# RWKV loop: identity products with a result in partitions 0 to 63 as TensorE transposes

## The reference, cut to what matters

```
def step(S, inp):
    r_t, w_t, k_t, v_t, kk_t, a_t = inp
    S = (S * w_t[:, :, None, :]
         - einsum('bhvk,bhk->bhv', S, kk_t)[..., None] * (kk_t * a_t)[:, :, None, :]
         + v_t[..., None] * k_t[:, :, None, :])
    return S, einsum('bhvk,bhk->bhv', S, r_t)
```

## Time and profile before

| what | us |
|---|---|
| median of 3 runs | 2818.54 |
| the runs | 2812.94 to 2820.93 |
| the profiled execution, its own time | 2810.1 |
| its span, first to last instruction | 2808.3 |

### The profile page before, as it was taken

The page is one execution under the profiler, slowest core; times in us unless marked ns, Lnnn a source line. Parts: engine busy times, 40 slices in busy tenths (PEclk is TensorE's granted clock), DMA queues, the critical chain, the costliest instruction groups (busy, mean ns, idle before and its releaser), DMA issues.

```text
span 2808.3 us, 63914 instructions
## 1 busy us (share of the span) xinstructions
PE 2549.5 (91%) x28913; PEld 2055.1 (73%) x28913; DVE 1173.8 (42%) x2014; ACT 558.0 (20%) x966; POOL 264.9 (9%) x166
## 2 busy tenths in 40 slices
PE   5899888999999979978888888888699999999993
PEld 3566556677776757747777777776599999999992
DVE  4434577544463376636655555627100000000004
ACT  3100221200010010024544444431200111011001
POOL 0000240000000000003333322210100000000001
PEclk9999999999999989979999999989799999999996
DMA  8554111312122013310000000002356555555553
GB/s 325 227 226 199 46 46 68 138 72 75 62 91 83 36 63 114 125 42 4 23 23 23 23 23 23 6 19 90 143 206 219 189 209 209 202 189 207 198 202 124
DMA packets 52552, 322.00 MB, mean 115 GB/s; under 512 B 8160, under 2 KB 10336, under 8 KB 21600
## 3 DMA queue, kind: packets, MB, share of 16 engines
q1 hardware_dynamic: 41824, 281.23, 27.4%
q10 hardware_dynamic: 7040, 20.45, 2.0%
q0 software_dynamic: 3456, 16.78, 1.5%
HBM read 289.07 MB, written 29.36 MB: 113 GB/s over the span
## 4 chain that ended last, share of the span: by engine, by line
PE 84%; DVE 7%; ACT 3%; issue 3%; DMA 2%; POOL 0%; SPq 0%; ACTq 0%; POOLq 0%; DVEq 0%
PE PS L877 35%; PE PS L1524 17%; PE PS L1539 8%; PE PS L1132 3%; PE PS L1265 3%; PE PS L1257 2%; PE PS L855 1%; PE PS L1197 1%; PE PS L1247 1%; PE PS L1329 1%; DMA arena<-in_k 1%; PE PS L598 1%; PE PS L1190 1%; ACT arena L1791 1%; PE PS L1224 1%
## 5 line engine op out<-in xcount | busy, mean ns | idle before, releaser
L877 PE MATMUL PS<-arena,ring 128*128 128x320 f32 x2680 | 752.0, 439 | 33.4 <-DVE arena L2389 12.3
L877 PEld LDWEIGHTS PS<-arena,ring 128*128 128x128 f32 x2680 | 512.6, 193 | 260.2 <-issue 24.7
L1524 PE MATMUL PS<-arena,ring 128*128 128x192 f32 x2816 | 465.5, 329 | 3.2 <-ACT arena L1906 3.2
L1524 PEld LDWEIGHTS PS<-arena,ring 128*128 128x128 f32 x2816 | 463.1, 192 | 4.2 <-ACT arena L1906 4.0
L1539 PE MATMUL PS<-arena,ring 128*128 128x192 f32 x1408 | 230.1, 326 | 0.0
L1539 PEld LDWEIGHTS PS<-arena,ring 128*128 128x128 f32 x1408 | 229.0, 190 | 0.0
L2639 DVE TENSOR_TENSOR arena<-arena,PS 128x192 f32<-128x192 f32 x88 | 31.2, 354 | 438.6 <-ACT arena L1912 438.6
L877 PE MATMUL PS<-arena 128*128 128x320 f32 x536 | 151.1, 432 | 0.0
L877 PEld LDWEIGHTS PS<-arena 128*128 128x128 f32 x536 | 101.8, 190 | 42.4
L796 POOL TENSOR_TENSOR arena<-arena,const 128x512 f32<-128x512 f32 (+1 forms) x24 | 26.2, 1091 | 1097.6 <-DVE arena L2490 765.2
L1265 PE MATMUL PS<-arena 64*64 64x64 f32 x3200 | 119.1, 220 | 10.9 <-issue 10.6
(11 more groups left out here) (331 smaller groups left out, 3130.6 us busy)
## 6 DMA issues: line engine op xcount, KB each, us to landing
ring<-in_k SPq DMA_DIRECT2D x145, 1024.0 KB, 4.8
arena<-in_k SPq DMA_DIRECT2D x48, 1024.0 KB, 9.1
ring<-in_exd SPq DMA_DIRECT2D x32, 1408.0 KB, 5.8
ring<-in_ffd SPq DMA_DIRECT2D x8, 1408.0 KB, 6.3
rkv_s<-arena ACTq DMA_DIRECT2D x24, 320.0 KB, 4.1
expert_rows<-arena POOLq DMA_DIRECT2D x4, 1536.0 KB, 10.3
x<-in_x SPq DMA_DIRECT2D x2, 2560.0 KB, 9.1
arena<-expert_rows ACTq DMA_DIRECT2D x8, 512.0 KB, 4.2
```

Source lines behind the costliest of these rows:

```text
L877: m = pe.matmul(out, lhs[:, k], rhs[:, k], start=k == 0, stop=k == count - 1)
L1524: m = pe.matmul(PS[:, k % 4, t * CAP:(t + 1) * CAP], w[:, kt, t * P:(t + 1) * P], xe[:, kt], start=kt == 0, stop=kt == KT - 1)
```

## The change

A helper `turned` sends an identity product to `pe.transpose` when its result lies in partitions 0 to 63, and to the same `pe.matmul` as before otherwise. It is put in for all four steps above. No wait, no buffer and no other engine's instruction is changed.

```diff
             wide = lambda b: psf[:, b * 512:b * 512 + TOK]
             eye_of = lambda hs: cst("eye64", hs)
 
+            def turned(out, rows, a, at):
+
+                if rows == heads[0]:
+                    return pe.transpose(out, a, eye_of(at))
+                return pe.matmul(out, a, eye_of(at), start=True, stop=True)
+
...
-                                m = pe.matmul(PS[token(c, h), b + r, k * HD:(k + 1) * HD], rkv[j % 2][hs, 2, c * HD:(c + 1) * HD], eye_of(hs), start=True, stop=True)
+                                m = turned(PS[token(c, h), b + r, k * HD:(k + 1) * HD], token(c, h), rkv[j % 2][hs, 2, c * HD:(c + 1) * HD], hs)
...
-                                    m = pe.matmul(PS[token(u, h), b + r, (2 * k + w) * HD:(2 * k + w + 1) * HD], KBf[hs, u, w], eye_of(hs), start=True, stop=True)
+                                    m = turned(PS[token(u, h), b + r, (2 * k + w) * HD:(2 * k + w + 1) * HD], token(u, h), KBf[hs, u, w], hs)
...
-                                m = pe.matmul(PS[hs, b + r, k * HD:(k + 1) * HD], QR[hs, u, 0], eye_of(hs), start=True, stop=True)
+                                m = turned(PS[hs, b + r, k * HD:(k + 1) * HD], hs, QR[hs, u, 0], hs)
...
-                            m = pe.matmul(PS[ts, 2 * i + r, k * HD:(k + 1) * HD], LTm[ts, 0, u], eye_of(ts), start=True, stop=True)
+                            m = turned(PS[ts, 2 * i + r, k * HD:(k + 1) * HD], ts, LTm[ts, 0, u], ts)
```

## The result

The changed kernel takes **3063.0 us**, the median of four runs (3057.1 to 3076.4), against 2816.4 for the kernel before on the same chip: a ratio of 1.0876, 95% interval [1.0856, 1.0897]. It is slower by 247 us, where 134 were forecast, and it lies above the range. The profiled execution took 3057.1 us, its span 3055.3.

The account below looks back on a forecast made before the run. PE was taken as the bound, at some 59 ns per pass of one array quarter. Changes of shape add 18.1 us per `j`, 145 in eight, less 11.7 of waits: 2818.5 + 134 = 2952 us, range 2920 to 3012.

Parts of the forecast that it names:

- the range: Whole kernel: the forecast's bounds, 2920 to 3012 us.
- The passes removed are worth nothing: In the four steps: removing 720 passes gains nothing, since the array quarters that stay set the same end.
- a quarter is the bound: In the four steps: each pass of one array quarter takes some 59 ns, and quarters run side by side.
- A transpose doesn't share the array with a 64*64 matmul: In the four steps: a 64x64 transpose runs as 64*128, so each change to or from a matmul is paid.
- Steps of under 60 ns: Sign of a wrong forecast: such steps between transposes and matmuls would make the time that of a rival.
- The first three rivals: Four steps: no shape change paid (2818 us, 0.10); saved passes count (2803, 0.05); serial, no change paid (2847, 0.06).
- The prices: Per `Q` pair 430 ns for 118, `KB` and `V` four 444 for 120, `first_inverse` four 618 for 236.
- the sum: RWKV loop: changes of shape add 18.1 us per `j`, 145 in eight, less 11.7 of waits, net +134 us.
- The waits: PE's waits for ACT's copies, 11.7 us, are swallowed; `var`'s (0.82) and `first_inverse`'s (0.55) stay.
- the clock falls: Rival, RWKV loop: mixed work at half clock adds some 100 us, 3050 us; chance 0.04.

Follow-up runs that it names:

- e11: Kernel before, matmuls only, products of each piece and of each `first_inverse` group sorted by array quarter: 2883.7 us, ratio 1.0250 to the kernel before.
- e2: The changed kernel in its order, each transpose replaced by a 128*64 matmul with half of the identity: 3089.1 us, ratio 1.0980 to the kernel before.
- e3: Kernel before with the transposes put into `Q` only: 2890.1 us, ratio 1.0263 to the kernel before.
- e4: Kernel before with the transposes put into `first_inverse` only: 2891.5 us, ratio 1.0269 to the kernel before.
- e9: The changed kernel with transposes in the third group alone (4 of the 20 units, none in `V`): 2877.8 us, ratio 1.0228 to the kernel before.
- e1: The changed kernel with all transposes of each piece and each `first_inverse` group issued before the matmuls: 2861.9 us, ratio 1.0174 to the kernel before.
- e7: Kernel before with transposes in `Q` only, ordered transpose, matmul, matmul, transpose: 2845.9 us, ratio 1.0114 to the kernel before.
- e8: Kernel before, no transposes, with products of `change_sides` put between those of `first_inverse`, behind each pair of units: 2806.4 us, ratio 0.9966 to the kernel before.
- e10: Like e8, but with those products ordered to visit the four array quarters in turn: 2806.2 us, ratio 0.9980 to the kernel before.
- e6: The changed kernel with each matmul that stays issued three times: 3263.8 us, ratio 1.1590 to the kernel before.

## Why the prediction was wrong, and where it was right

- **The passes removed are worth nothing: right, as far as the runs tell.** 720 records went, and nowhere did a stretch get shorter for it. e11 confirms by itself that a quarter is the bound: sorted by quarters, the same passes step at 58 to 59 ns, what the forecast read from 15 x 4 and 29.5 x 2.
- **A transpose doesn't share the array with a 64*64 matmul: right.** Steps of under 60 ns would have refuted it; they are 170 to 180 ns from a transpose to a matmul (1709.28 to 1709.45, 1717.44 to 1717.62). The first three rivals fall with this. The Trainium skill, page "TensorEngine Tiling (Array Packing)", section "Key Properties", says that a change of tiling mode drains TensorE; these steps agree, and so do the 0.15 us of e2 between two shapes of plain matmuls, though a step doesn't show what PE does in it. The Trainium skill, page "Perfetto Trace Analysis", section "Optimizing Tensor Performance", asks for a transpose wherever one is meant; here that costs 8.8%.
- **The prices: right.** 0.430, 0.444 and 0.618 us were forecast, 0.43, 0.44 and 0.60 are measured at full clock. With these the sum is 20 x 0.312 + 25 x 0.32 + 10 x 0.364 = 17.9 us per `j`, 143 in eight, less 12 of waits: 131 in place of 134.
- **The waits: right.** The waits for ACT's copies are gone, `var`'s and `first_inverse`'s stay (`var`'s is 0.5 us a time where 0.82 was forecast), DVE and ACT work as before.
- **The clock: wrong, and this is the step that failed.** The sum has no term for the clock: "the clock falls" stood among the rivals with a chance of 0.04, argued from the full clock over the loop of before with its waits. Of the 247 us, 131 are by the sum above the changes of shape; the other 116 are what is left for the clock. That size fits: a mean of 0.79 over 868 us is some 365 us at half, and work whose step grows from 0.44 to 0.66 loses a third of its time there, 122 us. The price named for that rival (100 us, 3050) was thus nearly right, and the range ended below it.

Why the argument failed: it took waits as the test for the clock. The loop of before had waits of up to 1.24 us and nearly always kept its clock, but nothing like 110 changes of shape per `j`, so its full clock spoke of a kind of work that the change was about to replace. The row also showed less than it was read for: its window ends at 1829 and the loop at 1887, its 1.00 hides one short fall, and behind it the last chain of the loop, between whose steps no pieces stand, ran at half clock. Windows of PE in the kernel before, that fall and that chain, then the same chain in the changed kernel:

```profile
1825.40:1828.80 3.40, 2.93 (x55) 0.50 0.50 154
1873.20:1886.80 13.60, 12.64 (x232) 0.50 0.03 8
```

```profile
2122.70:2134.00 11.30, 9.18 (x234) 1.00 0.03 9
```

All matmuls of this chain are 64*64, and its longest wait at half clock is 0.27 us (a wait of 1.40 us stands a little ahead of it). In the changed pieces PE is busy for 39.6 of 40.6 us by its records, and still is granted 0.70: a busy PE in this view isn't one that keeps its clock. The row that would have been nearest, the alternating L1509 and L1510 at half clock, was used for the price alone; it proves little, since that stretch began behind a wait of 21.6 us for a DMA.

What is shown: the clock falls in stretches with many changes of shape, with transposes (the change, e3, e4, e9) and without (e2); it does so far less with the same transposes and few changes (e1: 0.96, e7: 0.97), and hardly when one quarter works at a time in one shape (e11: 0.99). The Trainium skill, page "TensorE: Matmul & The Clock Gate", section "Part 4: PE-mode transpose", says that transposes don't count towards the clock as other work does. e2, without them at 0.85, and e1, with all of them at 0.96, show that transposes are neither needed for the low clock nor enough for most of it. Changes of shape aren't the only way to a lower clock: short falls stand in e8 and e10 without any, and the last chain of the kernel before is 13.6 us at half without any. But the order of the same instructions decides here between a loop at 0.96 (e1) and some 365 us at half (the change). What stays open is what in such a stretch the chip responds to: the change itself, or how little PE is given per microsecond around it. The changed `Q` leaves a record every 143 ns, e11's `first_inverse` one every 47, and the chain of before at half clock, without a change, one every 59. e6 doesn't decide it, since with three times the passes between changes it still leaves only one record every 60 ns in `KB` and, by the forecast's prices, every 95 in `Q`; the 13.55 us of changes at full clock in e2 leave one every 95. No run has passes as sparse as the change's in one shape, so neither reading is shown.

## What to carry to other kernels

In a stream of small matmuls, count the changes of tile shape before the passes: here one pass saved per product was worth nothing, each change some 0.1 us over the pass's own time, and sorting the same instructions by shape took back four fifths of the loss. Ask of a change that makes TensorE's work uneven what it does to the granted clock, and put that into the sum and the range rather than among the unlikely rivals: the low clock also lengthens the untouched work behind. Look at the clock over the whole loop before arguing from it, also where it falls for a few microseconds. Where products use only some quarters of the array, look for others that use the rest and lay them side by side (e8, e10).

## What was not expected of the hardware

- The clock fell to half in stretches where PE shows hardly any idle time (39.6 us busy of 40.6 at 0.70), and stayed there over dense matmuls of one shape: in e9 up to 1384, more than 13 us after the last transpose (1370.42).
- A change in the rows alone (128*64 against 64*64, e2) is paid like one between a transpose and a matmul: 0.15 us from one shape to the other, where that takes 0.17 to 0.18. (The whole run's 1.098 against 1.088 doesn't compare them, since e2's second passes are part of it.)
- Passes of one quarter step at 58 to 59 ns, and at a change of quarter a few of the next slip in beside them (mean 47 ns in e11), so the order within a piece need not alternate strictly to be fast.
